# Query products of the expert router: from split weights to whole single-precision weights

## The chip, the cores and the metric

The kernel runs on one core of one Trainium2 chip. The time is the device time of one execution in microseconds; the figure to predict is the median of several runs. A separate profiled execution gives the trace from which the rows below are taken.

Engines: PE is TensorE (matmuls), PEld its weight loads, DVE VectorE, ACT ScalarE, POOL GpSimd (it issues the indirect gathers), SP SyncE (it issues the plain transfers; SPq is its queue).

## What is computed

Two transformer blocks over 256 tokens of width 1024. The first ends in a routed layer of experts (PEER), and that part is what the change touches:

```python
def _peer(h, w_q, sub_keys_1, sub_keys_2, expert_u, expert_v):
    q = (h @ w_q).reshape(B, S, PEER_HEADS, PEER_DKEY)          # 1024 x 2048: 16 blocks of 128
    s1 = jnp.einsum('bshd,nd->bshn', q[..., :half], sub_keys_1)
    s2 = jnp.einsum('bshd,nd->bshn', q[..., half:], sub_keys_2)
    ...                                                          # top 16 of each, top 16 of the 256 sums
    u = expert_u[ix]                                             # (128 tokens, 8 heads, 16 rows, 1024)
    v = expert_v[ix]
    a = gelu(einsum('td,thkd->thk', hx, u)) * gx
    return einsum('thk,thkd->td', a, v)
```

The second block begins with a projection whose weights ("z") are loaded when the experts are done. In it `p @ w_ple` (the "pl" products) needs the embedding weights; they are computed in between the experts.

## The kernel before

**Stages.** Until about 300 us the first block's projections and attention run, with PE at work without a pause. Then, for tokens in two tiles t = 0, 1 of 128, eight heads each: 16 "heads" g = 0 to 15, and for each one 16 rows. One row j is a gather of 128 experts (one for each token), u and v together, 128 partitions x 2048 float32 = 1 MB. `rows[j]` are 16 buffers: 0 to 7 in the arena, 8 in `h_rows`, 9 to 15 in seven slots of `ring`. Every head uses the same 16 buffers.

**One pair of rows** passes through: gather (POOL, `gather`, line 659), two dots with the token's hidden vector (DVE, `dot_one`, line 2377), GELU and gate, then a diagonal matrix for each row (ACT, `weigh`, lines 1606, 1609, 1613), and four matmuls of diagonal times v, 128x512 float32 (PE, `head`, line 1109; called `values(p)` for head 0). The last of a row counts up `v_used`, on which POOL waits before it gathers the next head's row into the buffer (`pair`).

**Queries.** `wq` comes in eight chunks of 1 MB ("pq", numbers PQ to PQ+7), each for two of the 16 query blocks. Before the change a chunk is split as all others are: ACT copies it rounded to fp32r (`part`, line 1346), DVE subtracts to get the rest (`rest`, line 1959), and each k of a product is three fp32r matmuls (`three`, lines 770 to 772) of hi x hi, hi x lo and lo x hi. The input x2 is split the same way (`x2_hi`, `x2_lo`, `lo_of_x2`). A chunk so needs two buffers. They lie in `PQ_HOME`: either in row buffers of the arena ("row") or in the ring ("ring"), which the last row buffers share. Each block of queries is taken by ACT (`take_query`, line 1320), two blocks give the scores of a head (`head_scores`, lines 1066, 1071), DVE adds them up (`scores`), and picks the rows (`route` for heads 0 and 1, `top_keys`, `top_pairs`, `look_up` for head 2). `route(0, 0)` ends in line 2304, which frees POOL's first wait (`rows_ready`).

**Order.** Everything is written out by hand, engine by engine, and each engine works strictly in its own order; semaphores tie them. In this stage PE runs query(2) to query(15) with `head_scores` and `values` in between: values(0) follows query(7), values(1) and (2) follow query(9), values(3) follows query(10), values(4) follows query(15), and `head_scores(7)` comes before values(5) to (7). POOL begins in `first_rows`. SP issues the transfers of weights in one order; its loads of query chunks wait for the buffer to be free. The embedding weights (`in_pl_w`, `in_ple_t`) are issued when all queries and scores are done.

## Time and profile before

| | us |
|---|---|
| median of 3 runs | 1351.69 (1349.7 to 1352.07) |
| the profiled execution | 1353.7 |
| its span in the trace | 1352.0 |
| PE, DVE, ACT, POOL busy | 1215.2, 1059.7, 616.0, 290.1 |
| the granted PE clock, mean | 0.986 |
| queue q0 (gathers): bytes | 268.45 MB |

The span is divided in 40 slices of 33.8 us. Times in the trace count from the span's start. PE is busy nearly everywhere, but its busy share drops to 70 to 80% while the DMA moves 427 GB/s, and the other way round outside that stretch: the two lines have to be read together. In the views by windows, "DMA share" is the mean busy share of the 16 DMA engines (slightly over 1 where all are busy), and GB/s is what they moved.

### The profile page before, as it was taken

The page shows a single profiled execution, that of the slowest core. Times are in us where ns is not written, and L with a number is a line of the kernel's source. Part 1 is how long each engine was busy: PE and PEld are TensorE (multiplying, and loading weights), DVE is VectorE, ACT ScalarE, POOL GpSimd, SP SyncE. Part 2 cuts the span into 40 slices and gives each one's busy share as a digit, 9 for nine tenths or more (in the row PEclk, how much of TensorE's full clock was granted, in tenths as well). Part 3 has the DMA queues.
Part 4 walks back from the last instruction along what each step waited for, and adds up shares of the span by engine and source line. Part 5 has one row for each costly group of instructions (what it writes and reads, how often), then busy time and mean ns, then how long its engine had stood idle before and what let it go on. Part 6 is the DMA issues. An engine that isn't in the chain of part 4 may idle for free. (4 is left out here: it accounts for less than half of the span.)

```text
span 1352.0 us, 19494 instructions
## 1 busy us (share of the span) xinstructions
PE 1215.2 (90%) x6952; PEld 908.0 (67%) x6952; DVE 1059.7 (78%) x2161; ACT 616.0 (46%) x1265; POOL 290.1 (21%) x280
## 2 busy tenths in 40 slices
PE   7999999999989877778877777787899999999998
PEld 5999999999743333324332232333699999999998
DVE  7898678887879777777766777777699978898666
ACT  4666555656333333332433333233563265554445
POOL 1010000002545544344444434443000000000000
PEclk9999999999999999999999999999999999999999
DMA  9966446665999999999999999999853545454461
GB/s 388 384 225 249 187 158 235 245 234 234 375 422 426 427 428 428 427 427 427 427 427 427 427 428 428 428 427 428 341 187 126 187 137 183 180 187 173 174 236 43
DMA packets 55488, 416.64 MB, mean 308 GB/s; under 512 B 6113, under 2 KB 6753, under 8 KB 9202
## 3 DMA queue, kind: packets, MB, share of 16 engines
q0 software_dynamic: 37152, 268.45, 47.2%
q1 hardware_dynamic: 17792, 146.51, 29.3%
q8 instruction: 50, 0.82, 0.2%
q10 hardware_dynamic: 466, 0.63, 0.1%
q14 instruction: 28, 0.23, 0.0%
HBM read 414.52 MB, written 1.05 MB: 307 GB/s over the span
## 5 line engine op out<-in xcount | busy, mean ns | idle before, releaser
L1109 PE MATMUL ps<-arena 128*128 128x512 f32 x512 | 234.6, 603 | 57.0 <-ACT arena L1613 57.0
L1109 PE MATMUL ps<-ring,arena 128*128 128x512 f32 x440 | 214.1, 637 | 47.1 <-ACT arena L1613 47.1
L2377 DVE CUSTOM_DVE_ANT_0 arena<-arena 128x1024 f32<-128x1024 f32 x128 | 151.7, 1223 | 99.0 <-DMA arena<-in_experts,rowid 96.3
L1109 PEld LDWEIGHTS ps<-arena 128*128 128x128 f32 x512 | 92.7, 189 | 193.9 <-ACT arena L1613 98.0
L659 POOL DMA_INDIRECT arena<-in_experts,rowid x128 | 128.7, 1005 | 351.7 <-DVE rowid L2304 191.0
L1109 PEld LDWEIGHTS ps<-ring,arena 128*128 128x128 f32 x440 | 86.1, 202 | 170.4 <-issue 92.6
L772 PE MATMUL ps<-h_hi,w_lo 128*128 128x256 f32 x700 | 194.9, 278 | 0.0
L1606 ACT ACTIVATE arena<-arena 128x2 f32<-128x2 f32 x126 | 25.6, 203 | 369.1 <-DVE arena L2377 368.9
L770 PE MATMUL ps<-h_hi,w_hi 128*128 128x256 f32 x672 | 189.0, 281 | 3.0 <-DVE w_lo L1959 2.4
L771 PE MATMUL ps<-h_lo,w_hi 128*128 128x256 f32 x672 | 187.2, 279 | 0.0
L2377 DVE CUSTOM_DVE_ANT_0 ring<-ring,arena 128x1024 f32<-128x1024 f32 x112 | 133.3, 1222 | 35.4 <-DMA ring<-in_experts,rowid 26.5
L659 POOL DMA_INDIRECT ring<-in_experts,rowid x110 | 127.1, 1155 | 133.2 <-PE ps L1109 98.9
L1959 DVE TENSOR_TENSOR w_lo<-arena,w_hi 128x4096 fp32r<-128x4096 f32 (+1 forms) x30 | 122.1, 4069 | 29.7 <-ACT w_hi L1346 29.1
L1346 ACT ACTIVATE w_hi<-arena 128x4096 fp32r<-128x4096 f32 (+1 forms) x30 | 100.4, 3346 | 76.2 <-DMA arena<-in_up_w 32.1
L772 PEld LDWEIGHTS ps<-h_hi,w_lo 128*128 128x128 f32 x700 | 132.3, 189 | 0.0
L770 PEld LDWEIGHTS ps<-h_hi,w_hi 128*128 128x128 f32 x672 | 127.3, 190 | 4.1 <-DVE w_lo L1959 3.0
L771 PEld LDWEIGHTS ps<-h_lo,w_hi 128*128 128x128 f32 x672 | 127.1, 189 | 0.2
L770 PE MATMUL ps<-n_hi,e_hi 128*128 128x256 f32 (+1 forms) x352 | 101.4, 288 | 0.2 <-issue 0.2
L771 PE MATMUL ps<-n_lo,e_hi 128*128 128x256 f32 (+1 forms) x352 | 98.1, 279 | 0.0
L772 PE MATMUL ps<-n_hi,e_lo 128*128 128x256 f32 (+1 forms) x352 | 98.1, 279 | 0.0
L1959 DVE TENSOR_TENSOR e_lo<-ring,e_hi 128x2048 fp32r<-128x2048 f32 (+1 forms) x38 | 86.3, 2271 | 11.4 <-ACT e_hi L1346 10.8
L1613 ACT ACTIVATE arena<-ident,arena 128x128 f32<-128x128 f32 x252 | 85.4, 386 | 0.0
(424 smaller groups left out, 2558.4 us busy)
## 6 DMA issues: line engine op xcount, KB each, us to landing
ring<-in_early_w SPq DMA_DIRECT2D x43, 1024.0 KB, 5.0
arena<-in_ada_w SPq DMA_DIRECT2D x24, 1024.0 KB, 8.1
arena<-in_up_w SPq DMA_DIRECT2D x11, 2048.0 KB, 7.8
arena<-in_z_w SPq DMA_DIRECT2D x8, 2048.0 KB, 7.9
arena<-in_down_w SPq DMA_DIRECT2D x8, 1408.0 KB, 6.1
arena<-in_o_w SPq DMA_DIRECT2D x2, 2048.0 KB, 8.1
arena<-in_early_w SPq DMA_DIRECT2D x3, 1024.0 KB, 7.6
arena<-in_experts,rowid POOLq DMA_INDIRECT x128
```

The source lines that it names most:

```text
L659: pool.indirect_dma_start(out=rows[j], out_offset=None, in_=w["experts"], in_offset=bass.IndirectOffsetOnAxis(ap=rowid[:, even, j:j + 1], ...
L770: pe.matmul(out, hi[:, k, c0:c0 + m], x_hi[:, k, :], start=k == 0, stop=False, skip_group_check=True)
L771: pe.matmul(out, hi[:, k, c0:c0 + m], x_lo[:, k, :], start=False, stop=False, skip_group_check=True)
L772: return pe.matmul(out, lo[:, k, c0:c0 + m], x_hi[:, k, :], start=False, stop=k == KD - 1, skip_group_check=True)
L1109: mm = pe.matmul(BK[4 + 2 * t + b], diag[:, j, :], rows[j][:, D + b * 512:D + (b + 1) * 512], start=first and j == 0, stop=last and j == ( ...
L1346: act.activation(hi, whole, ACT.Copy).then_inc(S("w_hi"), 1)
L1606: act.activation(gel[:, even, two], dots[:, even, two], ACT.Gelu).then_inc(S("act_head"), 1)
L1613: act.activation(diag[:, j, :], ident[:, :], ACT.Copy, scale=amul[:, even, j:j + 1]).then_inc(S("diag"), 1)
L1959: v.tensor_tensor(lo, whole, hi.bitcast(F32), ALU.subtract).then_inc(S("w_lo"), 1)
L2377: v.tensor_tensor_reduce(out=u, in0=u, in1=h2tok[:, t, :], scale=1.0, scalar=0.0, op0=ALU.mult, op1=ALU.add, accum_out=dots[:, even, j:j + ...
```

## The change

The query weights are no longer split: each k of a query product is one float32 matmul on the chunk as it was loaded, and x2 is one float32 tensor. A chunk needs one buffer, so all eight have homes of their own: PQ, PQ+1, PQ+2 in the arena's row positions 8, 7 and 6 (position 8 is the place of the diagonal matrices), the others in ring slots 5, 2, 6, 0, 1. SP issues them in the order PQ+2, PQ+6, PQ+3, PQ+7, PQ+4, PQ+5 behind the other chunks and, right behind, the embedding weights, in a new place. The eight `part()` and `rest()` calls of the query chunks and `lo_of_x2` go. The ring slots of rows 9 to 15 are dealt out anew. POOL gathers in another order, and so do ACT and DVE for head 0: ACT weighs the pairs 4 to 7 later. Semaphore counts follow (`low_halves`).

```diff
-PQ_HOME = {PQ: ("row", 5, 6, None, None), PQ + 1: ("row", 7, 8, None, None), PQ + 2: ("row", 2, 3, None, None),
-           PQ + 3: ("ring", 0, 5, PQ - 4, PQ - 3), PQ + 4: ("ring", 1, 6, PQ - 3, PQ - 2),
-           PQ + 5: ("ring", 2, 4, PQ - 2, PQ - 1), PQ + 6: ("ring", 3, 5, PQ - 1, PQ + 3),
-           PQ + 7: ("ring", 0, 1, PQ + 3, PQ + 4)}
+PQ_HOME = {PQ: ("row", 8, None), PQ + 1: ("row", 7, None), PQ + 2: ("row", 6, None), PQ + 3: ("ring", 5, PQ - 3),
+           PQ + 4: ("ring", 2, PQ - 2), PQ + 5: ("ring", 6, PQ - 2), PQ + 6: ("ring", 0, PQ - 4),
+           PQ + 7: ("ring", 1, PQ - 3)}
+PQ_ORDER = [PQ + 2, PQ + 6, PQ + 3, PQ + 7, PQ + 4, PQ + 5]
...
-            x2_lo = over.enter_context(nc.sbuf_tensor("x2_lo", [P, KD, T + 2], F32R))
+            x2 = over.enter_context(nc.sbuf_tensor("x2", [P, KD, T + 2], F32))
...
-        in_ring = (6, 2, 4, 3, 5, 0, 1)
+        in_ring = (5, 3, 4, 2, 6, 0, 1)
...
-        ple_w, pleT = pacc, negdist[:, :, :]
+        ple_w, pleT = again(a_hT - 2 * D, NT, D), negdist[:, :, :]
...
-            for n in [*range(2, BB + 1), PQ, PQ + 1, *range(BB + 1, PQ), *range(PQ + 2, FIRST_C)]:
+            for n in [*range(2, BB + 1), PQ, PQ + 1, *range(BB + 1, PQ), *PQ_ORDER]:
...
-            sp.wait_ge(S("product"), BLOCK_AT[("pq", 15)] + 1)
-            sp.wait_ge(S("scores"), N_HEAD)
             sp.dma_start(ple_w.rearrange("p a b -> p (a b)"), w["pl_w"][0]).then_inc(S("p_in"), 16)
...
                 pool.wait_ge(S("rows_ready"), 1)
-                for j in (0, 1, 4, 5):
+                for j in range(6):
                     gather(j, 0)
                 pool.wait_ge(S("product"), BLOCK_AT[("pq", 5)] + 1)
-                for j in (2, 3, 6, 7):
+                for j in (6, 7, 10, 11):
+                    gather(j, 0)
+                pool.wait_ge(S("h2tok"), 4)
+                pool.wait_ge(S("product"), BLOCK_AT[("pq", 7)] + 1)
+                for j in (8, 9):
                     gather(j, 0)
                 pool.wait_ge(S("rows_ready"), 2)
-                pair(1, 1, 0)
-                pair(1, 1, 1)
-                pool.wait_ge(S("h2tok"), 4)
-                gather(8, 0)
-                pool.wait_ge(S("product"), BLOCK_AT[("pq", 9)] + 1)
-                gather(9, 0)
-                pair(1, 1, 2)
-                pair(1, 1, 3)
-                for p in (5, 6, 7):
-                    pool.wait_ge(S("product"), BLOCK_AT[("pq", 2 * p + 1)] + 1)
-                    for j in (2 * p, 2 * p + 1):
-                        gather(j, 0)
+                for p in range(4):
+                    pair(1, 1, p)
+                pool.wait_ge(S("product"), BLOCK_AT[("pq", 11)] + 1)
+                for j in (12, 13):
+                    gather(j, 0)
+                pool.wait_ge(S("product"), BLOCK_AT[("pq", 15)] + 1)
+                for j in (14, 15):
+                    gather(j, 0)
...
             def query(b):
-                product_parted(("pq", b), x2_hi, x2_lo, n=T + 2)
+                bank, whole = begin(("pq", b))
+                c0 = column(("pq", b))
+                for k in range(KD):
+                    mm = pe.matmul(bank[:, 0:T + 2], whole[:, k, c0:c0 + P], x2[:, k, :], start=k == 0, stop=k == KD - 1)
+                mm.then_inc(S("product"), 1)
```

The first two query products are written out in the same way, k by k for both, and wait for x2 alone. What DVE does for heads 0 to 2 keeps its parts, with `dot(0, 0, 0, 5)` and `(…, 6)` ahead of the scores beside them.

GpSimd, from its first gather on: rows in arena are rows 0 to 7 of a head, h_rows is row 8, ring rows 9 to 15. Before:

```order
L659 DMA arena<-in_experts,rowid 128x2048 x12
L659 DMA h_rows<-in_experts,rowid 128x2048
L659 DMA ring<-in_experts,rowid 128x2048
L659 DMA arena<-in_experts,rowid 128x2048 x4
L659 DMA ring<-in_experts,rowid 128x2048 x6
L659 DMA h_rows<-in_experts,rowid 128x2048
```

and after:

```order
L658 DMA arena<-in_experts,rowid 128x2048 x8
L658 DMA ring<-in_experts,rowid 128x2048 x2
L658 DMA h_rows<-in_experts,rowid 128x2048
L658 DMA ring<-in_experts,rowid 128x2048
L658 DMA arena<-in_experts,rowid 128x2048 x8
L658 DMA ring<-in_experts,rowid 128x2048 x4
L658 DMA h_rows<-in_experts,rowid 128x2048
```

Behind the first twelve rows now come the four pairs of head 1 in one piece (the second x8), and only behind them rows 12 to 15 (ring x4). Before, the pairs stood among the rows of head 0.

TensorE at the last query product. Before (the three forms of a k repeat eight times):

```order
L1066 MATMUL ps<-keyT,arena 128x128 x2
L1071 MATMUL ps<-keyT,arena 128x128 x4
L770 MATMUL ps<-x_hi,pq_ring 128x258
L771 MATMUL ps<-x_lo,pq_ring 128x258
L772 MATMUL ps<-x_hi,pq_ring 128x258
```

and after, with the values of pair 4 behind it:

```order
L1067 MATMUL ps<-keyT,arena 128x128 x2
L1072 MATMUL ps<-keyT,arena 128x128 x4
L1126 MATMUL ps<-x,ring 128x258 x8
L1117 MATMUL ps<-h_rows,arena 128x512 x2
L1117 MATMUL ps<-ring,arena 128x512 x2
```

A product is 8 matmuls instead of 24; what stands around it has not moved.

ScalarE around the taking of the last query (258 columns); line 1589, now 1598, copies a shifted score, 1606 and 1615 begin the weights of a pair. Before:

```order
L1320 ACTIVATE arena<-ps 128x258
L1589 ACTIVATE arena<-ps 128x256
L1606 ACTIVATE arena<-arena 128x2
L1609 ACTIVATE arena<-arena 128x1 x2
L1613 ACTIVATE arena<-ident,arena 128x128 x2
L1562 ACT_TABLE_LOAD
L1562 ACTIVATE arena<-arena 128x16
L1606 ACT_TABLE_LOAD
L1606 ACTIVATE arena<-arena 128x2
```

and after:

```order
L1598 ACTIVATE arena<-ps 128x256
L1615 ACTIVATE arena<-arena 128x2
L1618 ACTIVATE arena<-arena 128x1 x2
L1622 ACTIVATE arena<-ident,arena 128x128 x2
L1332 ACTIVATE arena<-ps 128x258
L1615 ACTIVATE arena<-arena 128x2
L1618 ACTIVATE arena<-arena 128x1 x2
L1622 ACTIVATE arena<-ident,arena 128x128 x2
```

The weights of one pair (4) now stand ahead of the last query's copy and those of the next right behind it.

## Rows read from the trace of the kernel before

**Rows 1.** The page: slices of PE and of the DMA's GB/s, and the gather queue (packets, MB, share).

```profile
PE   7999999999989877778877777787899999999998
...
GB/s 388 384 225 249 187 158 235 245 234 234 375 422 426 427 428 428 427 427 427 427 427 427 427 428 428 428 427 428 341 187 126 187 137 183 180 187 173 174 236 43
...
q0 software_dynamic: 37152, 268.45, 47.2%
```

**Rows 2.** Windows: length, busy PE, PEld, DVE, ACT, POOL, PE clock, DMA share, GB/s.

```profile
308.00:316.00 8.00, 8.00 (x66) 7.90 (x66) 7.79 (x34) 6.54 (x8) 0.00 (x0) 1.00 0.00 0
...
346.50:349.50 3.00, 3.00 (x10) 1.40 (x9) 2.75 (x5) 0.95 (x1) 2.50 (x2) 1.00 0.49 123
346.50:360.00 13.50, 13.50 (x77) 9.99 (x76) 12.47 (x30) 5.95 (x12) 10.59 (x7) 1.00 0.86 300
360.00:384.45 24.45, 21.42 (x144) 18.00 (x143) 12.80 (x34) 6.85 (x21) 10.89 (x10) 0.96 1.01 427
316.00:384.45 68.45, 64.74 (x424) 53.28 (x423) 50.80 (x130) 30.51 (x74) 32.41 (x26) 0.99 0.94 379
384.45:400.00 15.55, 13.98 (x30) 5.59 (x30) 13.86 (x31) 6.67 (x23) 7.82 (x6) 0.96 1.01 414
...
400.00:940.00 540.00, 430.77 (x943) 175.44 (x942) 406.17 (x1054) 186.89 (x627) 237.68 (x227) 0.97 1.01 427
```

**Rows 3.** Timeline of GpSimd's gathers, 346 to 379 us: start, length, waited for.

```profile
346.69 0.94 POOL L659 DMA_INDIRECT arena<-in_experts,rowid  x1 [6.33 <-PE ps L1109]
...
374.42 0.93 POOL L659 DMA_INDIRECT ring<-in_experts,rowid  x1 [4.92 <-PE ps L772]
...
378.39 1.74 POOL L659 DMA_INDIRECT h_rows<-in_experts,rowid  x1 [1.80 <-PE ps L1109]
```

**Rows 4.** Timeline of SyncE's queue: last "wo" chunk, query chunks, embedding weights.

```profile
278.60 0.33 SPq L541 DMA_DIRECT2D ring<-in_early_w  x1
281.13 0.33 SPq L536 DMA_DIRECT2D arena<-in_early_w  x1
...
330.93 0.33 SPq L536 DMA_DIRECT2D ring<-in_early_w  x1
388.17 0.33 SPq L600 DMA_DIRECT2D arena<-in_pl_w  x1
```

**Rows 5.** Timeline of PE, from the first query product past the last.

```profile
300.17 0.28 PE L770 MATMUL ps<-x_hi,pq_row 128*128 128x258 f32 x1
...
305.93 0.95 PE L844 MATMUL ps<-ones,h_rows 128*128 128x1 f32 x8
...
342.18 7.22 PE L1109 MATMUL ps<-arena 128*128 128x512 f32 x16 [0.68 <-ACT arena L1613]
348.83 0.69 PE L770 MATMUL ps<-x_hi,pq_ring 128*128 128x258 f32 x1
...
373.98 1.88 PE L1109 MATMUL ps<-h_rows,arena 128*128 128x512 f32 x4
...
377.41 0.61 PE L1066 MATMUL ps<-keyT,arena 128*128 128x128 f32 x4
```

**Rows 6.** Timeline of PE: float32 products of 256 columns, two records each.

```profile
14.76 5.77 PE L863 MATMUL ps<-xT,ones 128*128 128x256 f32 x26
...
25.03 5.42 PE L871 MATMUL ps<-sq,ring 128*128 128x256 f32 x24 [0.46 <-DMA ring<-in_early_w]
```

**Rows 7.** Timeline of DVE: row numbers, a split, a dot.

```profile
316.53 0.17 DVE L2304 CAST rowid<-arena 128x16 uint32<-128x16 f32 x1
...
344.14 2.29 DVE L1959 TENSOR_TENSOR pq_ring<-ring,pq_ring 128x2048 fp32r<-128x2048 f32 x1
...
378.09 1.22 DVE L2377 CUSTOM_DVE_ANT_0 ring<-ring,arena 128x1024 f32<-128x1024 f32 x1 [7.14 <-DMA ring<-in_experts,rowid]
```

**Rows 8.** Timeline of ACT: the first and the last step of a pair's weights.

```profile
350.05 0.20 ACT L1606 ACTIVATE arena<-arena 128x2 f32<-128x2 f32 x1 [2.61 <-DVE arena L2377]
...
350.68 0.69 ACT L1613 ACTIVATE arena<-ident,arena 128x128 f32<-128x128 f32 x2
```

More of the change, by code:

```diff
@@ L200, in halves, with low_halves @@
     return sum(n for _, n in HALVES[:names.index(stage)]) + k + 1
+def low_halves(stage, k=0):
+    names = [name for name, _ in HALVES]
+    return halves(stage, k) - (KD if names.index(stage) > names.index("n2") else 0)
 def norm_count(tag):
@@ L463, in parts, with query_chunk @@
             return raw[:, r, 0:n], hi[:, 0:n], w_lo[:, r, 0:n]
+        def query_chunk(c):
+            where, at_home, _ = PQ_HOME[c]
+            return pq_raw[where][:, at_home, :]
         def by_block(a, n=512):
@@ L522, in load_early @@
                 if n in PQ_HOME:
-                    where, _, _, before, _ = PQ_HOME[n]
-                    if n < PQ + 2:
+                    before = PQ_HOME[n][2]
+                    if before is None:
                         sp.wait_ge(S("dsa_cp"), AH)
                         sp.wait_ge(S("ada_dot"), 2 * ADA_HALVES)
-                    elif where == "row":
-                        sp.wait_ge(S("taken_V"), taken_by("V", BLOCK_AT[("bb", 7)]))
                     else:
@@ L1036, in _ @@
                 head_turn(h)
-            pe.wait_ge(S("x_lo"), halves("ba"))
+            pe.wait_ge(S("x_lo"), low_halves("ba"))
             for b in range(8):
@@ L1084, in _ @@
             pe.wait_ge(S("small_in"), 48)
-            abreast("pq", 2, x2_hi, x2_lo, "n2", n=T + 2)
+            first = [begin(("pq", b)) for b in range(2)]
+            for k in range(KD):
+                pe.wait_ge(S("x_hi"), halves("n2", k))
+                for b in range(2):
+                    mm = pe.matmul(first[b][0][:, 0:T + 2], first[b][1][:, k, b * P:(b + 1) * P], x2[:, k, :],
+                                   start=k == 0, stop=k == KD - 1, skip_group_check=True)
+                    if k == KD - 1:
+                        mm.then_inc(S("product"), 1)
             norm2_sums()
@@ L1549, in _ @@
             act.activation(d_hi[:, :, :], dsaT[:, :, :], ACT.Copy).then_inc(S("x_hi"), 1)
-            for _ in range(5):
+            for _ in range(3):
                 part()
@@ L1629, in _ @@
             take_query(2)
-            part()
             take_query(3)
-            part()
             take_query(4)
@@ L2426, in _ @@
             both_scores(1)
-            rest()
             soft_weights(0, 0)
```

86 lines of the change are left out of this document (31 added, 55 removed).

## The prediction

> **What bounds the kernel now.** I read the slices first. From slice 10 to slice 27, roughly 340 to 945 us, the DMA engines move 422 to 428 GB/s while TensorE's busy share drops to seven or eight tenths [rows 1]. These are the 256 gathers of expert rows. One stretch gives the ceiling: 427 GB/s from 400 to 940 us with the DMA share at 1.01 and PE busy 430.77 of 540 us [rows 2]. The gather queue moves 268.45 MB [rows 1], so one row (1.0486 MB) costs 1.0486 / 0.427 = 2.457 us. Until the last row has landed nothing behind it can finish, so this stretch ends at its start, plus its bytes over 427 GB/s, plus whatever time the DMA stands short of rows. A change matters by three things only: when rows begin, what else is carried among them, and gaps. Ahead of it PE sets the pace: the DMA moves nothing from 308 to 316 us while PE is busy throughout [rows 2].
>
> Second, how close to empty the transfers run at the start. From 346.5 us the DMA falls to 300 GB/s until 360 us, and is back at 427 from 360 to 384.45 [rows 2]. The hole of 346.5 to 360 us costs 13.5 x (427 - 300) / 427 = 4.0 us. The rows read by the PE products of values free buffers only then: the gather at 346.69 had waited 6.33 us for line 1109 [rows 3].
>
> Third, the other bytes among the rows: the last query chunk is issued at 330.93, the embedding weights (1024 KB) at 388.17 with their input (128x2x256 float32, 256 KB) behind them [rows 4]. That is 1.049 + 1.311 MB, 2.25 rows, 5.5 us.
>
> **The change part by part.**
>
> *Bytes moved ahead.* In the changed order no query chunk waits for anything later than a product of the third "wo" chunk or the landing of an earlier query chunk, and the embedding weights follow at once. Before, the third was issued at 281.13 and only the eighth at 330.93 [rows 4]; now all are issued by about 296, plus 1.3 MB, and from 308 us to 316 the DMA moved nothing [rows 2], so there is room for them. Worth: all of the 5.5 us. They share the DMA with the last "wo" chunk (issued at 278.60 [rows 4], used in the last 5.5 us of PE before 300.17, from 294.7); two chunks together need 2 x 2.46 us plus some 2 us, so it lands near 286, and its split takes 2.3 us on VectorE [rows 7] and about as much on ScalarE ahead of it: 4 us to spare. I take zero.
>
> *Splits removed.* Eight times 2.3 us on VectorE go [rows 7], and a copy of the same size on ScalarE, and eight VectorE halves of x2. PE runs without a gap through this stretch (from 300.17 to 373.98, but for 0.68 us before 342.18) [rows 5], so none of it was waited for. Zero by itself.
>
> *Query products dearer on PE.* Three fp32r matmuls of 258 columns start every 0.12 us, 24 of them 2.88 us for a product: the first two products take 305.93 - 300.17 = 5.76 us [rows 5]. One float32 matmul is two records; 24 records of 256 columns took 5.42 us and 26 took 5.77, which after 0.2 us of pipeline tail is 0.43 us for each matmul [rows 6]. At 258 columns: 0.433 us, 3.47 us for a product. Sixteen products: 16 x 0.59 = 9.4 us more. Off go the dips where PE turned from float32 values to fp32r queries (the first query record behind values at 348.83 lasts 0.69 us instead of 0.28, 0.4 us more [rows 5]; it comes twice, and about 0.1 us at five other places): 1.3 us; and the idle 0.68 us. The sum is 7.4 us; adding the pieces in order (with the score and value products at their old durations) gives 7.7. The last query product ends at 373.98 + 7.7 = 381.7.
>
> *What hangs on it.* GpSimd issues in program order. Rows 14 and 15 wait for the last query product, since chunks 6 and 7 lie in their buffers; every later gather stands behind them. Before, row 14 was issued at 374.42, 0.44 us behind the product [rows 3]. Now: 382.15. By that time 22 rows have been issued: twelve of head 0 (0 to 11), eight of head 1 behind four pairs of values, and rows 12 and 13. Can they keep the DMA busy till then? The first two products cost 1.2 us more, so the row numbers come at 317.7 instead of 316.53 [rows 7] and the stream starts 1.2 us later, at an effective 321.0 (before: 25.94 MB by 384.45, worked back, gives 319.8). 22 rows last until 321.0 + 22 x 2.457 = 375.1. Transfers of a row issued on an empty queue come up about 2.3 us later: after the issue at 346.69 the window 346.5 to 349.5 carries 123 GB/s, that is 2.1 us lost [rows 2, 3]. So the DMA stands still from 375 to 382.15 + 2.3 = 384.45. **The gap of 9.4 us is the price of the change, and the old holes lie inside it.**
>
> *The balance at 384.45.* After: 22 rows landed, 234 to come, nothing else. Before: 68.45 us x 379 GB/s = 25.94 MB [rows 2], less the query chunk 24.89 MB = 23.74 rows; 232.26 to come, and 1.25 rows' worth of embedding weights: 233.51. The changed kernel is behind by 0.49 rows, 1.2 us. Before then lost another 15.55 x (427 - 414) / 427 = 0.5 us by 400 us [rows 2], which the changed one need not lose in that form. So +0.7 us.
>
> *Is there a second gap?* Rows 14 and 15 last until 389.4. The next pair needs the values of pair 4. Its weights are made on ScalarE ahead of taking the last query, in 1.3 us (350.05 to 351.37 [rows 8]), and the dots of rows 8 and 9 are done by 363 (they stand behind the scores of head 4, on PE until 358.4), so PE goes on without a stop: 381.7 + 3.5 = 385.2, issue 0.8 us later (before, 377.41 to 378.39, about 1 [rows 3, 5]), stream at 388.3: no gap. The next pairs follow at 3.5 us each against 4.9 us of DMA, so the queue fills up. But it is thin for some 12 us. From 349.5 to 360 us, also with one to three rows queued, the DMA gave (13.5 x 300 - 3 x 123) / 10.5 = 351 GB/s, 18% short [rows 2]. Bounds for 384.45 to 396: nothing, or 0.18 x 11.5 = 2.1 us. I take 0.8, below the middle, because in the old stretch the issues themselves came late, at the pace at which values freed buffers, and here four of them come within 6 us.
>
> The Trainium skill ("DMA: Bandwidth & Descriptors", Anatomy of one DMA, SWDGE (gpsimd) path) gives a gather a fixed part of about 2.0 us besides bytes over 436 GB/s, and under Bandwidth 341 GB/s for single transfers of 1 MB. By that the thin stretch would lose 2.3 us. The trace's 351 GB/s agrees for a thin queue, its 427 for a full one does not show the fixed part at all.
>
> *Reordering of heads 0 and 1.* Dots, scores and look-ups change places on VectorE, but it has idle time (7.14 us before the dots at 378.09 [rows 7]) and the gap is set by PE. Zero. The second half of the program, and the last rows of the stream, are as before.
>
> Sum: +1.2 - 0.5 + 0.8 = **+1.5 us**. The profiled execution took 1353.7 us and would take 1355.2; the median of the three runs is 1351.69, so I forecast **1353.2 us**. For this kernel 0.2% is 2.7 us, about what a measurement can tell from no change.
>
> **The rivals.**
> (a) *Thin queue*, the slower one. After the gap transfers run at 351 GB/s till about 400 us: 0.18 x 16 = 2.9 us instead of 0.8, +3.6 us, 1355.3. For it: 346.5 to 360 us. Against it: PE frees buffers faster than the DMA fills them. The rule of the skill named above would lead here. It decides if the windows between 385 and 400 us are below 400 GB/s.
> (b) *PE waits for something before its last query*, for instance for the take of a product three blocks back, which stands on ScalarE behind weights that wait for dots. Every us adds one, since the gap hangs on this product alone. Against it: the nearest case is the values of pair 3, on PE from 358.4; rows 6 and 7 land by some 344 and their weights are ready near 349, so it takes 9 us of delay. 4 us of such a wait would give 1357.2.
> (c) *No gap*. If the float32 product costs PE no more than its three parts did, the last query ends near 374 and rows are there at about 376.7: 7.7 us less, 1345.5. Against it: two independent rows at 0.43 us a matmul.
> (d) *It does not do what it says*: the stretch ends by something else than bytes, and the time stays at 1351.7. Against it: 427 GB/s for 540 us.
>
> **How the numbers follow.** Forecast 0.50 (1350.5 to 1356 by itself: the thin queue's bounds, 0.8 us on the last product, 0.4 us on the start-up of a transfer, 1 us of measurement); (a) 0.20; (b) 0.12; (c) 0.11, in parts too (half the gap, 1349); (d) 0.07. Outside 1348.5 to 1358.0 lie most of (c) and the far part of (b). Faster by over 0.2%: (c) and a little of the forecast, 0.17. Slower by over 0.2%: nearly all of (a), (b) and a tenth of the forecast, 0.36. Within: 0.47.
>
> **What would show it.** Right: query products of about 3.5 us, the last ending near 381.7; the gather of row 14 half a us behind it; DMA at nothing for 8 to 10 us before 384.5 and 427 GB/s soon after; no embedding weights among the rows; the stream's end within 3 us of before. Wrong: no hole near 380 (then c), a last query later than 383 (b), or 350 GB/s till 400 (a).

## The result and the profile after

The changed kernel took 1354.40 us, the median of 22 runs (1352.67 to 1362.22); the kernel before, run beside it, 1351.38 us (22 runs, 1349.68 to 1353.23). The ratio is 1.0028, with a 95% interval from 1.0018 to 1.0037: 3.8 us slower by the ratio (2.4 to 5.0), 3.0 by the medians. The profiled execution took 1352.67 us, its span 1350.9 us; it is the fastest of the 22. Some runs of either kernel lie 5 to 8 us above its others (three of these 22, and six of 26 of the kernel before beside the first four experiments), which moves a median of a dozen runs by about a microsecond, and one run of the kernel before in its repeat (before_again), at 3533 us and a granted clock of 0.36, is left out of its median.

The page of the changed kernel (slices of DMA GB/s, gather queue), beside [rows 1]:

```profile
GB/s 388 388 223 252 185 159 233 245 278 242 416 305 416 427 427 428 427 427 427 427 428 427 427 427 427 428 428 427 381 164 150 187 129 183 188 187 171 177 236 42
...
q0 software_dynamic: 37152, 268.45, 47.3%
```

The gather queue carries the same 268.45 MB. The slices 8 and 9 carry more than before (278 and 242 against 234 and 234): the bytes moved ahead. Slice 10 has lost its hole (416 against 375), and slice 11 has a new one (305 against 422). Windows of the changed kernel (length, busy PE, PEld, DVE, ACT, POOL, PE clock, DMA share, GB/s), beside [rows 2]:

```profile
308.00:316.00 8.00, 8.00 (x44) 7.13 (x43) 7.04 (x34) 4.38 (x7) 0.00 (x0) 1.00 0.01 2
316.00:384.45 68.45, 68.45 (x323) 54.01 (x322) 45.21 (x131) 24.37 (x69) 23.76 (x24) 1.00 0.82 338
346.50:360.00 13.50, 13.50 (x51) 8.51 (x50) 5.70 (x24) 3.78 (x10) 3.76 (x4) 1.00 1.01 426
360.00:375.00 15.00, 15.00 (x71) 12.23 (x70) 10.47 (x29) 3.03 (x7) 4.38 (x4) 1.00 1.00 404
375.00:380.00 5.00, 5.00 (x31) 4.52 (x30) 2.77 (x5) 1.92 (x7) 0.00 (x0) 1.00 0.18 74
380.00:385.00 5.00, 5.00 (x19) 3.25 (x18) 1.77 (x5) 2.32 (x7) 1.88 (x2) 1.00 0.17 26
384.45:400.00 15.55, 13.43 (x37) 6.41 (x36) 8.20 (x15) 6.81 (x20) 6.82 (x7) 0.89 1.00 402
400.00:420.00 20.00, 18.87 (x45) 8.00 (x43) 17.92 (x56) 6.39 (x26) 12.48 (x11) 1.00 0.99 405
400.00:940.00 540.00, 432.28 (x951) 176.79 (x950) 408.16 (x1062) 188.48 (x633) 243.24 (x228) 0.98 1.01 426
```

The DMA runs full to about 375 us and does next to nothing until 384.5, while TensorE is busy in every microsecond from 308 to 384.45. Whoever reads only busy shares sees an engine at work; the GB/s column, together with GpSimd's wait of 14.01 us in the rows below, shows that it is the one that all wait for.

Timelines of the changed kernel: TensorE (its first query products, the last, the first values behind it, the last pair of head 0), GpSimd (rows 0 and 14, pairs 4 and 7), VectorE (row numbers), SyncE (the last query chunks, embedding weights, embeddings), beside [rows 3 to 5, 7]:

```profile
299.94 7.13 PE L1090 MATMUL ps<-x,arena 128*128 128x258 f32 x32
...
378.87 3.65 PE L1126 MATMUL ps<-x,ring 128*128 128x258 f32 x16
382.36 1.88 PE L1117 MATMUL ps<-h_rows,arena 128*128 128x512 f32 x4
...
396.29 5.40 PE L1117 MATMUL ps<-ring,arena 128*128 128x512 f32 x8 [2.12 <-ACT arena L1622]
```

```profile
317.97 1.09 POOL L658 DMA_INDIRECT arena<-in_experts,rowid  x1 [182.68 <-DVE rowid L2293]
...
382.80 0.94 POOL L658 DMA_INDIRECT ring<-in_experts,rowid  x1 [14.01 <-PE ps L1126]
...
386.77 0.94 POOL L658 DMA_INDIRECT h_rows<-in_experts,rowid  x1 [1.78 <-PE ps L1117]
...
402.50 1.41 POOL L658 DMA_INDIRECT ring<-in_experts,rowid  x1 [5.05 <-PE ps L1117]
```

```profile
317.51 0.17 DVE L2293 CAST rowid<-arena 128x16 uint32<-128x16 f32 x1
```

```profile
286.14 9.36 SPq L537 DMA_DIRECT2D ring<-in_early_w  x5
295.55 0.58 SPq L599 DMA_DIRECT2D arena<-in_pl_w  x1
296.18 0.44 SPq L600 DMA_DIRECT2D negdist<-in_ple_t  x1
```

A query product takes 382.36 - 378.87 = 3.49 us, and the last one ends at 382.36. GpSimd had waited 14.01 us for it when it issued row 14 at 382.80.

### The profile page after: what moved, and what is told of

Read it like the earlier page. It is cut to its first block and busy times, and to the rows that moved or that the text cites. A ratio compares the mean times of both kernels' runs of the same rounds, so it can differ in the third digit from the quotient of the medians.

```text
span 1350.9 us, 19203 instructions
## 1 busy us (share of the span) xinstructions
PE 1219.7 (90%) x6824; PEld 908.2 (67%) x6824; DVE 1039.4 (77%) x2144; ACT 602.3 (45%) x1257; POOL 286.0 (21%) x280
## 3 DMA queue, kind: packets, MB, share of 16 engines
q0 software_dynamic: 37152, 268.45, 47.3%
HBM read 414.52 MB, written 1.05 MB: 308 GB/s over the span
## 5 line engine op out<-in xcount | busy, mean ns | idle before, releaser
L1117 PE MATMUL ps<-ring,arena 128*128 128x512 f32 x440 | 211.0, 630 | 44.6 <-ACT arena L1622 44.6
```

The costliest lines, as they stand in the source:

```text
L1117: mm = pe.matmul(BK[4 + 2 * t + b], diag[:, j, :], rows[j][:, D + b * 512:D + (b + 1) * 512], start=first and j == 0, stop=last and j == ( ...
```

## The experiments

Twelve runs follow the result, two of them repeats of the two kernels. Three measures are given of each. One is the timed runs, as a ratio to the kernel before on the same chip. The second is from the trace: **the last group of values before the gate** on TensorE, that is, its last 16 records of 512 columns (eight matmuls, two records each: rows 10 to 13 of the last head). It cannot start before 252 of the 256 rows have landed, and nothing of the program's second half is in it. Of the first profiles of the kernel before and of the changed one (start, length, line):

```profile
956.86 7.13 PE L1109 MATMUL ps<-ring,arena 128*128 128x512 f32 x16 [1.22 <-ACT arena L1613]
```

```profile
958.39 7.13 PE L1117 MATMUL ps<-ring,arena 128*128 128x512 f32 x16 [1.23 <-ACT arena L1622]
```

The third is **the 240th row**: the time at which packets worth 240 rows have ended on the gather queue.

The row numbers, which start the stream, come at 317.4 to 318.8 us from one profile to the next with the changed query products. The two columns headed "against the changed kernel" take that out: mark minus row numbers, against the mean of the two profiles of the changed kernel (640.85 for the last group; 604.2 for the 240th row, from 604.5 and 603.9).

| kernel | row numbers | last group | against the changed kernel | 240th row, against the changed kernel | median us | ratio to before (95%) |
|---|---|---|---|---|---|---|
| before | 316.53 | 956.86 | -0.5 | -1.2 | 1351.38 | |
| before_again | 316.77 | 955.59 | -2.0 | -2.0 | 1351.35 | 1.0008 (0.9993 to 1.0023) |
| changed | 317.51 | 958.39 | 0 | +0.3 | 1354.40 | 1.0028 (1.0018 to 1.0037) |
| after_again | 318.11 | 958.92 | 0 | -0.3 | 1355.43 | 1.0017 (0.9998 to 1.0035) |
| weights_late | 317.42 | 961.34 | +3.1 | +2.8 | 1356.98 | 1.0047 (1.0030 to 1.0064) |
| products_shorter | 317.89 | 953.82 | -4.9 | -5.9 | 1349.04 | 0.9982 (0.9963 to 1.0001) |
| row14_early | 318.43 | 958.63 | -0.6 | -0.2 | 1354.21 | 1.0031 (1.0011 to 1.0051) |
| eight_more_before_product15 | 317.89 | 963.28 | +4.5 | +3.7 | 1359.97 | 1.0055 (1.0030 to 1.0080) |
| eight_more_behind_values7 | 318.78 | 962.41 | +2.8 | +1.6 | 1354.78 | 1.0025 (1.0012 to 1.0038) |
| own_buffer | 317.46 | 956.89 | -1.4 | -1.2 | 1355.22 | 1.0008 (0.9991 to 1.0026) |
| own_buffer_values_first | 317.57 | 964.06 | +5.6 | +5.9 | 1360.42 | 1.0062 (1.0042 to 1.0082) |
| own_buffer_pairs_between | 317.57 | 960.45 | +2.0 | +0.9 | 1355.15 | 1.0019 (1.0002 to 1.0035) |
| pairs_between_weights_first | 317.81 | 955.39 | -3.3 | -2.6 | 1351.59 | 1.0008 (0.9996 to 1.0020) |
| product15_before_values6 | 317.62 | 955.78 | -2.7 | -3.2 | 1350.76 | 1.0012 (0.9996 to 1.0028) |

The two marks differ by up to 1.2 us, and the traces show where that comes from. From the 40th row to the 240th the stream takes 491.0 to 491.1 us in all fourteen profiles. But the last group does not wait for a count of bytes; it waits until a pair of rows has landed whole, and a pair's landing is spread out. Each gather counts its semaphore up in 16 steps, which the trace has one by one. The 32 steps of one pair, about 605 us behind the row numbers, stretch over 6.1 and 6.7 us in the two profiles of the changed kernel and over 7.7 and 6.7 us in those of the kernel before (about 100 us behind the row numbers: 3.7 and 3.6, 5.8 and 4.8). So this spread differs by up to 1.0 us between two executions of the same kernel. The 240th row is the sharper mark for what happens at the gap, the last group the one on which the end of the program depends.

### What a byte costs ahead of the rows and among them

```diff
+            sp.wait_ge(S("product"), BLOCK_AT[("pq", 15)] + 1)
+            sp.wait_ge(S("scores"), N_HEAD)
             sp.dma_start(ple_w..., w["pl_w"][0])
             sp.dma_start(pleT, w["ple_t"]...)
```

> The changed kernel with one edit: the two embedding transfers (1.31 MB) wait again for the last query product and all scores, so they run among the rows of head 1. Theory (bytes): what stands ahead of the stream costs nothing there, among the rows it costs its bytes, 1.31 MB by 427 GB/s = 3.1 us; so 3.1 us slower than the changed kernel (1357.5 by its median of 1354.4), with the last group of values before the gate at 961.5 instead of 958.4. Rival (the rows of head 1 leave the queue idle enough around 385 to 400 us to take them): under 1 us slower. Rival (the early weights themselves delayed the query chunks or the first rows): not slower, or faster.

The last group came at 961.34, 3.07 us later from the row numbers, the 240th row 2.8 us later, and the median rose by 2.6 us. 1.31 MB over 427 GB/s is 3.07 us. The theory holds: among the rows these bytes cost their time at 427 GB/s, ahead of the stream they do not, and the thin queue behind the gap did not hide them.

### Whether TensorE makes the gap

```diff
-                for k in range(KD):
+                for k in range(KD - 1):
                     mm = pe.matmul(bank[:, 0:T + 2], whole[:, k, c0:c0 + P], x2[:, k, :], ...)
```

> The changed kernel with the last of the eight k-steps left out of query products 2 to 15 (the queries are incomplete, so other rows are chosen and the output is another; everything else is issued as before). 14 products are 0.44 us shorter each, 6.1 us in all. Theory (TensorE sets the issue of rows 14 and 15 and of pairs 4 to 7, the DMA queues wait): the last query product ends near 376.3 instead of 382.4, row 14 is issued near 376.7, the gap behind 375 us shrinks from 9.4 to about 3.5 us, and the kernel is 6 us faster than the changed one (1348.4). Rival (the stream is bound by its bytes and its thin queue, TensorE is covered): 0 to 1 us faster.

Timeline of GpSimd (row 14), then windows of 375 to 385 us, both of this kernel:

```profile
377.06 0.93 POOL L658 DMA_INDIRECT ring<-in_experts,rowid  x1 [11.82 <-PE ps L1126]
```

```profile
375.00:385.00 10.00, 10.00 (x38) 5.94 (x37) 5.49 (x11) 6.05 (x16) 4.19 (x4) 1.00 0.69 233
```

From the row numbers, row 14 came at 59.17 us instead of 65.29: 6.12 us earlier, as 14 x 0.44 says. The window lost 10 x (427 - 233) / 427 = 4.5 us instead of 8.8. The last group moved by 4.9 us, the ratio by 0.0046 (6 us, though the two ratios come from different chips). By the 240th row it is 5.9 us of the 6.1. So TensorE's time ahead of product 15 goes into the gap one for one, and the last group's 4.9 is short by the spread of the landings (7.7 us here, 6.1 and 6.7 in the changed kernel). The rival (0 to 1 us) falls. The other way round, eight matmuls more ahead of product 15:

```diff
             head_scores(6)
+            e = ...
+            pe.wait_ge(S("taken_" + e), ...)
+            repeated(8)
             query(15)
             values(4)
```

> The changed kernel with eight more float32 matmuls of a query product's form ahead of query product 15, into its bank (results overwritten, the output is whole). Theory: TensorE sets the issue of rows 14 and 15 and of all pairs behind them, so its 3.5 us come through one for one: row 14 is issued at 386.3 instead of 382.8, and the kernel is 3.5 us slower than the changed one. Rival (thin queue, or bytes alone): 0 to 1 us slower.

```profile
386.67 0.94 POOL L658 DMA_INDIRECT ring<-in_experts,rowid  x1 [17.50 <-PE ps L1126]
```

Row 14 at 68.78 us from the row numbers, 3.49 later; the last group 4.5 us later, and against after_again on the same chip the ratio 0.0038 higher (5 us). The 240th row came 3.7 us later. One for one, for the issue and for the stream: theory right in its size too, and what the last group shows beyond that is again the spread of the landings (7.4 us here). As a control eight of the same form, with another weight tile, stood where TensorE was taken to have slack:

```diff
             for p in range(5, PAIRS):
                 values(p)
+            repeated(8)
```

> The changed kernel with eight more float32 matmuls of 258 columns (3.5 us) behind the values of pair 7 of head 0 instead of ahead of product 15 (result overwritten nowhere needed; the output is whole). Theory: there TensorE has waits of 1 to 2 us per pair from 410 us on, and rows are in the queue until about 410 us, so it takes back its 3.5 us before the queue runs dry: 0 to 1 us slower than the changed kernel, where the same eight ahead of product 15 cost 4.5 us by the last group of values. Rival (TensorE's time costs wherever it stands before 410 us): 3.5 us slower.

By the last group that cost 2.8 us, by the 240th row 1.6 (1.3 and 1.9 against the two profiles of the changed kernel), neither the 0 to 1 of the theory nor the rival's 3.5; by the median next to nothing (1354.78 against 1354.40 and 1355.43 of the changed kernel). The window behind the gap:

```profile
400.00:420.00 20.00, 20.00 (x55) 10.33 (x54) 18.20 (x56) 5.62 (x24) 8.99 (x8) 0.98 0.98 384
```

384 GB/s is 2.0 us lost between 400 and 420 us, where the changed kernel's first profile lost 1.0 and its second nothing. TensorE is busy in all 20 us there, so the slack that I read from its waits behind 410 us was too late to help. About half of the eight matmuls' 3.5 us came through to the stream. TensorE still sets the pace behind 400 us, but not one for one any more.

### Buffers or order

If TensorE's total work up to head 1 sets the gap, then freeing a buffer earlier gives almost nothing. First the row whose buffer is free at product 13:

```diff
-                pool.wait_ge(S("product"), BLOCK_AT[("pq", 15)] + 1)
-                for j in (14, 15):
-                    gather(j, 0)
+                pool.wait_ge(S("product"), BLOCK_AT[("pq", 13)] + 1)
+                gather(14, 0)
+                pool.wait_ge(S("product"), BLOCK_AT[("pq", 15)] + 1)
+                gather(15, 0)
```

> The changed kernel with one edit: row 14 is gathered behind query product 13, which frees its buffer, and only row 15 waits for product 15. Theory (TensorE's order sets the gap): row 14 comes 8 us earlier, but the next free buffers behind row 15 are those of pair 4, which are free only after the values at 382 to 386 us, so the hole is only cut in two; what is gained is the thin queue between 384 and 400 us, 0.9 us at most: 0 to 0.9 us faster than the changed kernel. Rival (the buffers of the last two chunks cause the gap): one row of 2.46 us less in the gap, 2.5 us faster.

Row 14 was issued at 375.41, and the hole was cut in two. Windows of this kernel:

```profile
375.00:380.00 5.00, 5.00 (x30) 4.54 (x29) 2.04 (x3) 1.63 (x7) 0.94 (x1) 1.00 0.95 352
380.00:385.00 5.00, 5.00 (x20) 3.60 (x19) 2.48 (x7) 2.09 (x9) 0.93 (x1) 1.00 0.03 13
384.45:400.00 15.55, 15.55 (x46) 7.61 (x45) 10.45 (x21) 8.99 (x28) 7.54 (x8) 1.00 0.86 295
```

One row fills 375 to 380 us, and behind 384.45 the DMA gives 295 GB/s instead of 402: nearly the same bytes by 400 us. 0.6 us by the last group, 0.2 by the 240th row, nothing by the median. The rival (2.5 us) falls. Then the whole of it, with a buffer for the last chunk:

```diff
-           PQ + 7: ("ring", 1, PQ - 3)}
+           PQ + 7: ("own", 0, None)}
...
+        own_chunk = flat_at(a_hT - HALF, HALF)
...
-            sp.dma_start(ple_w..., w["pl_w"][0])
             sp.dma_start(pleT, ...)
+            sp.wait_ge(S("product"), BLOCK_AT[("pq", 15)] + 1)
+            sp.dma_start(ple_w..., w["pl_w"][0])
...
-                for j in (6, 7, 10, 11):
+                for j in (6, 7, 10, 11, 15):
...
-                pool.wait_ge(S("product"), BLOCK_AT[("pq", 15)] + 1)
-                for j in (14, 15):
-                    gather(j, 0)
+                pool.wait_ge(S("product"), BLOCK_AT[("pq", 13)] + 1)
+                gather(14, 0)
```

> The changed kernel with a buffer of its own for the last query chunk (in the place of the 1.05 MB embedding weight, loaded behind product 15), row 15 gathered with rows 6 to 11, row 14 behind product 13; the order on TensorE is untouched. Theory (TensorE's order makes the gap): rows in the queue last until 380, the weight fills 384 to 386.5, pair 4 is issued at 386.8 as before, so the hole is as long as it was, less what the weight fills, and the end of the rows of head 0 to 2 is the same but for the thin queue: 0.5 to 1.5 us faster than the changed kernel. Rival (the buffers held by the last two chunks make the gap): two rows of 2.46 us more ahead of the gap, less the 2.5 us of weight: 2.5 us faster; with the weight in the gap 4.9 us faster.

The last group came 1.4 us earlier and the 240th row 1.2, inside the 0.5 to 1.5 us of the theory; the ratio is 0.0009 below after_again's. Pair 4 was issued at 386.72 as before. Both rivals (2.5 and 4.9 us) fall: the buffers of the last two chunks are not what sets the size of the gap.

What is left is the order on TensorE. Moving values ahead of products does not make TensorE's work less, so there is a floor. 32 rows and the 1.05 MB of weight last from 321.0 to 321.0 + 32 x 2.457 + 2.5 = 402. The next buffer comes free with the first pair of head 1. In the changed kernel TensorE reaches that head's values at 401.52 after 2.12 us of waiting, so without any wait it would be done with the pair near 403, whatever the order, and the new row's data come some 2.5 us later. (It is an estimate, and 1.7 us too late: in that profile the pair ahead took 5.40 us instead of 3.70, at a lower granted clock, as the section on the prediction shows.) What can be won is the rest of the 9.7 us of gap and the thin queue behind it. Four attempts followed, on the buffer of own_buffer. The first two on TensorE:

```text
 own_buffer_values_first             own_buffer_pairs_between
   query(13) values(4)                 query(13) values(4)
   head_scores(6) values(5)            head_scores(6) values(5)
   query(14) values(6) values(7)       query(14) values(6)
   query(15) head_scores(7)            query(15) head_scores(7) values(7)
```

In both, ScalarE makes the weights of pair 4 ahead of its take of product 13, those of pair 5 ahead of product 14 and those of pairs 6 and 7 ahead of product 15, and VectorE adds up the scores of head 7 only behind the dots of pair 7.

> A version built on the theory that TensorE's order and the buffer of the last chunk make the gap. The last query chunk has a buffer of its own (in the place of the 1.05 MB embedding weight, which is loaded behind product 15; the 0.26 MB of embeddings stay early), row 15 is gathered with rows 6 to 11 and row 14 behind product 13; on TensorE the values of pairs 4 and 5 stand ahead of query product 14 and those of 6 and 7 ahead of product 15. Theory: rows in the queue last until 389.8 us, then 1.8 us of gap until pair 6, and 2.5 us for the weights among the rows, 4.3 us in all against 9.4 us of gap and 0.9 us of thin queue: 5 to 6 us faster than the changed kernel (1349), 2 to 3 us faster than the kernel before. Rival (the gap is filled anyway by what comes later, or ScalarE and VectorE become late in the new order): within 1 us of the changed kernel.

> As own_buffer_values_first, but the scores of head 7 stand ahead of the values of pair 7 again, since VectorE takes them before the first dots of head 1: there the dots of head 1 began at 403.0 us instead of 395.4, its values at 406.8 instead of 401.5, and the queue ran dry from 403 to 415 us. Theory: the scores of head 7 end near 398.5, the first values of head 1 start near 402 as in the changed kernel, the second gap goes, and what is left is about 5 us of gaps in all: 2 to 3 us faster than the changed kernel. Rival (the order costs TensorE itself more than it gives): slower than it still.

The first was 5.6 us slower than the changed kernel, and badly foreseen. Timeline of VectorE (scores of head 7, first dot of head 1), then of GpSimd (first gather for head 2):

```profile
401.59 1.00 DVE L1927 SCALAR_TENSOR_TENSOR arena<-ps,csil,arena 128x256 f32<-128x256 f32 x2 [14.33 <-PE ps L1075]
402.97 1.23 DVE L2370 CUSTOM_DVE_ANT_0 arena<-arena 128x1024 f32<-128x1024 f32 x1 [0.38 <-DVE arena L1927]
```

```profile
413.38 1.66 POOL L662 DMA_INDIRECT arena<-in_experts,rowid  x1 [14.54 <-PE ps L1120]
```

VectorE stood 14.33 us in front of the scores of head 7, which I had put last on TensorE, with all dots of head 1 queued behind. GpSimd then waited 14.54 us for a freed buffer. The hole was in part moved, from 375 to 403 us, and the whole of it grew. Windows of this kernel:

```profile
375.00:403.00 28.00, 23.43 (x87) 14.29 (x85) 8.16 (x18) 7.97 (x23) 9.72 (x9) 1.00 0.89 334
403.00:415.00 12.00, 8.18 (x15) 3.57 (x16) 11.20 (x27) 3.80 (x15) 1.61 (x1) 0.72 0.47 195
```

28 x 93 / 427 = 6.1 us are lost in the first and 12 x 232 / 427 = 6.5 us in the second. The second version mended that and was still 2.0 us slower than the changed kernel by the last group, 0.9 by the 240th row. TensorE's timeline (values of pairs 5 and 6, first values of head 1) names the cause:

```profile
379.81 3.70 PE L1120 MATMUL ps<-ring,arena 128*128 128x512 f32 x8 [0.77 <-ACT arena L1626]
...
388.73 3.70 PE L1120 MATMUL ps<-ring,arena 128*128 128x512 f32 x8 [1.73 <-ACT arena L1626]
...
403.39 14.00 PE L1120 MATMUL ps<-arena 128*128 128x512 f32 x32 [1.83 <-ACT arena L1626]
```

0.77 + 1.73 + 1.83 = 4.3 us of waiting for line 1626, the last step of a pair's weights on ScalarE. The weights of pair 6 stood there behind the take of product 14, which itself waits for TensorE. That is a queueing mistake of mine, not the theory's, so the third version only moved them:

```diff
+            weigh(0, 5, 0)
             take_query(13)
             copy_shifted(6)
-            weigh(0, 5, 0)
             soften(2)
             act.preload_act_table(ACT.Gelu)
+            weigh(0, 6, 0)
             take_query(14)
-            weigh(0, 6, 0)
             weigh(0, 7, 0)
```

> As own_buffer_pairs_between, with ScalarE in another order: the weights of pairs 4 and 5 ahead of its take of product 13, those of pair 6 ahead of its take of product 14. In that run TensorE waited 0.8 and 1.7 us for ScalarE, which stood behind the take of product 14 with dots that were ready 5 us earlier. Theory: the values of pair 6 end near 389 instead of 392.3, the scores of head 7 near 394.5 instead of 398, the first values of head 1 start near 399.5 instead of 403.4; gaps of 1.9 and 1.5 us and 2.5 us of weight remain against 10.3 us in the changed kernel: the last group of values before the gate near 954.5 us, 4 us faster than the changed kernel and 2 us faster than the kernel before. Rival (TensorE's total work, not the order, sets the time): the last group at 957.5 or later.

955.39 instead of the 954.5 expected, 3.3 us ahead of the changed kernel from the row numbers, with the median at 1351.59 and the ratio at 1.0008. The rival (957.5 or later) falls. But I had forecast it 2 us faster than the kernel before, and it is not: that one's own last group turned out to lie lower than its first profile said (next). The fourth attempt is one more exchange, product 15 ahead of the values of pair 6 (ScalarE takes it ahead of the weights of pair 7):

> As pairs_between_weights_first, with query product 15 ahead of the values of pair 6 and the scores of head 7 between these and the values of pair 7. In that run TensorE waited 0.6 us for ScalarE ahead of the scores of head 7 and 1.8 us ahead of the first values of head 1, whose dots stand on VectorE behind these scores. Theory: the scores begin at 393.1 instead of 393.75, their wait goes, the values of head 1 start 0.7 us earlier (399.9), pair 6 is issued 3.5 us later (gap about 390 to 395.5, of which the 1.05 MB weight fills 2.5 us): the last group of values before the gate 0 to 1 us earlier than 955.4 us, the time within 1 us of that run (1351.6). Rival (the later issue of pair 6 counts whole): 3 us slower than it.

955.78, and 1350.76 us with a ratio of 1.0012: the same within what can be told. The first values of head 1 started at 399.54 instead of 400.60, as foreseen, and pair 6 was issued 3.3 us later, which took it back. By the timed runs neither version beats the kernel before (1.0008 and 1.0012, both intervals with 1 inside); both win back about what the change costs.

### The two kernels again

> The changed kernel itself once more, as the measure for the three kernels beside it. Theory: gap from 375 to 384.5 us, last group of values before the gate near 958.4 us, 1.5 us later than in the kernel before (956.9), and 1 to 3 us slower than that by the timed runs. If the first profile of the changed kernel was an unusual one, the group comes at another time, by more than 1 us.

> The kernel before itself once more, for a second profile. Theory: up to the end of the rows it is as in the first profile (row numbers at 316.5, last group of values at 956.9 us); its tail from there to the first output transfer took 390.7 us in the first profile, against 388.1 to 388.8 in four profiles with the changed query products, whose tail has the same instructions, so that was chance: it is near 388.7 in about half of the profiles. Rival (the tail itself is faster with the embedding weights at the new place): 390.7 again.

From the row numbers to the last group the changed kernel takes 640.88 and 640.81 us, the kernel before 640.33 and 638.82. That the first two agree is in part chance, since the 240th row lies 0.55 us apart in them and the spread of the landings makes up for it; in the kernel before it lies 0.8 us apart, and the spread adds to it. Windows of its second profile, beside the rows of 346.5 and of 384.45 in [rows 2]:

```profile
346.50:360.00 13.50, 13.50 (x77) 9.91 (x76) 12.47 (x31) 6.14 (x12) 10.39 (x7) 1.00 0.87 317
384.45:400.00 15.55, 12.90 (x27) 5.41 (x26) 14.21 (x36) 7.62 (x26) 6.15 (x6) 0.89 1.01 421
```

Its old hole costs 3.5 us here, not 4.0, and the stretch up to 400 us loses 0.2 us, not 0.5. The tail, from the last group to the first output transfer, was 390.7 us in the first profile and 388.8 in the second, where the theory said 388.7 and the rival 390.7 again. So the profiled execution that I had argued from was late twice, by 1.3 us in the stream and by 2.0 us behind it, and it is no property of the kernel. The 2.0 us have a place in the trace. The windows of 1160 to 1170 us of the first profile, then of the second:

```profile
1160.00:1170.00 10.00, 9.90 (x73) 9.91 (x73) 9.18 (x15) 4.25 (x5) 0.00 (x0) 0.83 0.46 188
1160.00:1170.00 10.00, 10.00 (x91) 10.00 (x90) 9.24 (x13) 5.39 (x5) 0.00 (x0) 1.00 0.39 165
```

In the first the granted clock is at half for 3.4 us from 1160.7 on. From the first "up" transfer to the first "down" one it took 125.6 us, the second 123.6. The same fall at the same stage stands in five of the fourteen profiles; four of them take 125.6 us over this stretch (the fifth, own_buffer, 128.5), the nine others 123.6 to 124.0.

## Why the prediction was right, and where a size was off

The forecast of 1353.2 us came within 1.2 us of the median and well inside the range of 1348.5 to 1358.0, and the mechanism held, step by step. The difference between the kernels was forecast as +1.5 us and measured as 3.0 to 3.8, about twice that.

- **Bytes.** All chunks and both embedding transfers were issued by 296.18, and in the old stretch from 308 to 316 us the DMA was idle. weights_late gives their price among the rows, 3.1 us for 1.31 MB. The 427 GB/s of the prediction is the right exchange rate.
- **Splits.** Their removal was taken as worth nothing by itself. No kernel tests it alone; what supports it is that TensorE was busy throughout before, but for 0.68 us, and is now.
- **The float32 product.** 3.49 us against 3.47. The last one ended at 382.36 against 381.7. From the first product on, TensorE needs 82.42 us instead of 73.81, 8.6 more instead of 7.7: 16 x 0.61 = 9.8 us for the products, less the 0.68 of idle time, which leaves 0.5 us for the dips. They were credited with 1.3, the one part of this step that was too large.
- **What hangs on it.** Row 14 was issued 0.44 us behind the product, at 382.80 (382.15); rows began 1.0 us later than before (1.2), and 22 rows lasted until about 375. Between 346.5 and 385 us the DMA lost 13.5 x 1 / 427 + 15 x 23 / 427 + 5 x 353 / 427 + 5 x 401 / 427 = 9.7 us, against 9.4.
- **The balance at 384.45.** 68.45 x 338 GB/s = 23.14 MB, 22.06 rows, against 22. products_shorter and eight_more_before_product15 show that this gap moves with TensorE's work, and row14_early and own_buffer that the stream's end hardly moves with the buffers.
- **The thin queue.** This is the term of the sum that was mis-sized. I took 0.8 us, with bounds of 0 and 2.1. The changed kernel's first profile lost 15.55 x 25 / 427 = 0.9 us before 400 and 20 x 22 / 427 = 1.0 before 420, together 1.9. In after_again the row numbers come 0.60 us later, so its windows have to start 0.60 us later too:

```profile
385.05:400.60 15.55, 13.67 (x41) 6.58 (x40) 8.41 (x18) 6.86 (x21) 6.35 (x7) 1.00 1.00 390
400.60:420.60 20.00, 17.26 (x41) 7.22 (x39) 17.89 (x54) 6.42 (x26) 12.49 (x12) 1.00 1.01 427
```

  That is 15.55 x 37 / 427 = 1.3 us, all of it ahead of 400.6. Part of the reason for more than 0.8 is pair 7. I had argued for a value below the middle because four issues come within 6 us, and overlooked that its gather has to wait: its dots need row 15, the last row behind the gap. Changed kernel, first profile (VectorE, then windows), and after_again (TensorE, GpSimd, windows):

```profile
392.44 1.23 DVE L2366 CUSTOM_DVE_ANT_0 ring<-ring,arena 128x1024 f32<-128x1024 f32 x1 [3.72 <-DMA ring<-in_experts,rowid]
396.00:400.00 4.00, 3.71 (x5) 1.65 (x6) 4.00 (x7) 1.51 (x6) 1.22 (x1) 0.57 1.01 422
404.00:406.00 2.00, 2.00 (x6) 0.94 (x5) 1.60 (x6) 0.52 (x2) 1.01 (x2) 1.00 0.87 320
```

```profile
396.65 3.70 PE L1117 MATMUL ps<-ring,arena 128*128 128x512 f32 x8 [1.88 <-ACT arena L1622]
...
401.16 1.96 POOL L658 DMA_INDIRECT ring<-in_experts,rowid  x1 [3.35 <-PE ps L1117]
...
396.60:400.60 4.00, 3.95 (x9) 1.82 (x10) 3.96 (x10) 1.31 (x6) 0.98 (x1) 1.00 1.00 416
```

  In both profiles the gather waits for the values of pair 7. In the first the granted clock falls to 0.57 on the mean of 396 to 400 us, behind 2.12 us in which TensorE stood idle; the pair's values take 5.40 us, the gather comes at 402.50, and a second, smaller hole opens (320 GB/s from 404 to 406 us). In after_again TensorE stood idle for 1.88 us, the clock stays at 1.00, the values take 3.70 us, the gather comes at 401.16 (1.9 us earlier from the row numbers), and behind 400.6 us nothing is lost. So the size of this term depends on the execution: 1.9 us in one, 1.3 in the other.
- **The kernel before.** I credited 0.5 us for its dip before 400 us; in its second profile that is 0.2.

With both, the sum is +1.2 - 0.2 + 1.9 = +2.9 us in place of +1.5, or +2.3 with the 1.3 us of after_again, and the medians say 3.0. The last groups say +1.5 in the first pair of profiles and +3.3 in the second; the first agrees with the forecast only by chance. The 240th row, on which the spread of the landings has no part, came 2.5 us later in the first pair and about 3.0 in the second. The result is thus between the forecast and rival (a), whose own number, 1355.3, is a little nearer to the median of 1354.4. Rival (a) was to be told by windows below 400 GB/s between 385 and 400 us. They read 402 in one profile and 390 in the other, so by that sign it is undecided; but its mechanism, 351 GB/s up to 400 us and 2.9 us lost, is in neither. That the forecast number was met with one term at about half its size is helped by a base that was a little high: the median of three before was 1351.69, that of 22 is 1351.38.

Rivals (b) and (c) are out: TensorE did not stop before its last query, and the gap is there. Rival (d) is out by weights_late and products_shorter, which moved the end of the rows by the bytes and by TensorE's time.

One part of the method was weak. A single profile stood for the kernel before, and what differs between two executions of it (1.3 us by the last group, 3.3 us by the whole span) is as large as the effect that I forecast or larger.

## What to carry to other kernels

Where a stream of transfers bounds the time, count how many of them can be issued before the engine that frees their buffers gets to its next release; if that runs out, everything this engine does ahead of the release costs one for one (here 5.9 of 6.1 us and 3.7 of 3.5), and an engine that is busy without a gap while the transfers stand still is the sign of it. A buffer given back earlier, or an issue moved up, only moves the hole as long as that engine's total work is the same; the order of its work helps only when every in-order engine beside it is reordered too, or its waits eat the gain, as 4.3 us did here. To tell a few microseconds apart, compare a mark in the trace that the edit must move with the mark that starts the stretch, choose it as near behind the edit as the steady stream allows (here the 240th row rather than the last group), shift the windows of two profiles by their starts before their GB/s are compared, and take two profiles of each kernel.

## What the runs showed of the hardware

TensorE's pace in the second half of the program varies by as much as the effect studied, and the granted clock in the records tells only part of it. The profiled execution of own_buffer took 1359.6 us although its last group, at 956.89, came 1.5 us ahead of the changed kernel's. It lost its time in the "up" and "down" stages. Windows of 1250 to 1300 us, of after_again and then of own_buffer:

```profile
1250.00:1300.00 50.00, 50.00 (x443) 50.00 (x442) 29.51 (x33) 21.94 (x22) 0.00 (x0) 1.00 0.52 182
```

```profile
1250.00:1300.00 50.00, 50.00 (x427) 50.00 (x426) 30.01 (x34) 18.62 (x20) 0.00 (x0) 1.00 0.49 174
```

Both are busy throughout at a granted clock of 1.00, but the one starts 443 matmuls and the other 427, 3.6% fewer. From the first "up" transfer to the first "down" one it took 128.5 us, against 124.0 in after_again, and from there to the gate's 69.3 against 66.6, so the lower count is not a matter of records missing from the trace. In 10 us windows the lower pace (87 or 88 matmuls instead of 90 or 91) begins just behind a window with a granted clock of 0.83, at 1160 to 1170 us, and lasts to the end of the rows that I looked at. The first profile of the kernel before has the same dip at the same place and goes back to 91. The dip by itself costs 2.0 us (125.6 against 123.6 us); the lower pace behind it costs 128.5 - 125.6 = 2.9 us in this stretch and 2.6 in the next. What decides between the two I did not find. Together they account for this run's extra time and have the size of the other late runs of both kernels, though only this one was caught in a profile.

The other point is how steady the gather stream is once it is full: 427 GB/s from 420 to 940 us in all fourteen profiles, 2.455 us for each row from the 40th to the 240th, at a mean granted TensorE clock of 0.97 or 0.98. What is not steady is when a single pair has landed whole: the steps of its semaphore stretch over 3.6 to 5.8 us about 100 us into the stream and over 6.1 to 7.7 us about 600 us into it, in the four profiles of the two kernels.
